# Gate projections of tiles 12 to 23 as 2x2 blocks of seven products, with the pieces of a two-layer hybrid decoder step placed anew

## What is computed

```
h = rmsnorm(x, norm_g)
proj = h @ w_in                     # columns are split into
qkv_a, z_a, beta, alpha, f_b, z_b, qkv_c, z_c, gate_raw = split(proj)
o_a = gated_delta(qkv_a, ...) * silu(z_a)     # branch A
o_b = rwkv7(f_b, ...) * silu(z_b)             # branch B
o_c = block_attention(qkv_c, cache) * silu(z_c)   # branch C
up = einsum(stack(o_a, o_b, o_c), w_branch)
gates = sigmoid(gate_raw + b_gate)            # 3 x 1024 columns
x = x + sum_over_branches(gates * up) @ w_out
x = x + sigmoid(x @ w_pg + b_pg) * (ple @ w_ple)
```

## Time and profile before

| | |
|---|---|
| Median of three runs | 1141.0 us (1139.41 to 1143.78) |
| The profiled execution | 1139.07 us, its span 1137.2 us |
| TensorE busy | 1111.2 us, 98% of the span |
| VectorE busy | 647.6 us, 57% |
| ScalarE busy | 343.8 us, 30% |
| Chain that ended last, by engine | TensorE 86%, VectorE 8% |
| Granted TensorE clock, mean | 0.999 |

### The profile page before, as it was taken

One profiled execution on the slowest core, in us unless ns is written; L12 is line 12 of the kernel. 1 busy time (PEld: TensorE's weight loads), 2 busy tenths in 40 slices (PEclk: granted clock), 3 DMA queues, 4 the chain that ended last, 5 costly groups with the idle time before them and its releaser, 6 DMA issues.

```text
span 1137.2 us, 22007 instructions
## 1 busy us (share of the span) xinstructions
PE 1111.2 (98%) x8504; PEld 867.1 (76%) x8504; DVE 647.6 (57%) x1478; ACT 343.8 (30%) x773; POOL 129.4 (11%) x215
## 2 busy tenths in 40 slices
PE   7999999999999999999999999999999999999998
PEld 6778777768777777779977777777777777777897
DVE  4566546766666505257556673766667643251856
ACT  1243223321334154210323332233224332433013
POOL 0211402020211000000011123201102011000000
PEclk9999999999999999999999999999999999999999
DMA  8733236422513674444346331654134157634431
GB/s 262 222 112 117 56 99 209 104 76 62 121 46 93 205 258 149 152 155 129 106 149 191 105 99 43 191 160 93 39 90 136 39 138 248 198 121 153 145 111 43
DMA packets 162323, 148.51 MB, mean 131 GB/s; under 512 B 41513, under 2 KB 144527, under 8 KB 162029
## 3 DMA queue, kind: packets, MB, share of 16 engines
q1 hardware_dynamic: 156820, 135.99, 40.1%
q0 software_dynamic: 2848, 7.79, 2.1%
q10 hardware_dynamic: 2552, 3.32, 0.9%
HBM read 135.42 MB, written 11.07 MB: 129 GB/s over the span
## 4 chain that ended last, share of the span: by engine, by line
PE 86%; DVE 8%; issue 2%; DMA 2%; ACT 1%; SPq 1%; DVEq 0%; ACTq 0%
PE psum L1250 51%; PE psum L1291 10%; PE psum L1178 5%; PE psum L1480 1%; PE psum L1463 1%; PE psum L1338 1%; PE psum L1599 1%; DMA arena<-conv_in 1%; PE psum L1865 1%; PE psum L1814 1%; PE psum L1683 1%; DVE arena L2641 1%; DVE arena L2796 1%; PE psum L1844 1%; PE psum L1699 1%
## 5 line engine op out<-in xcount | busy, mean ns | idle before, releaser
L1250 PE MATMUL psum<-x_a,ring 128*128 128x288 f32 x1120 | 293.7, 411 | 0.0
L1250 PE MATMUL psum<-x_b,ring 128*128 128x288 f32 x1120 | 293.7, 411 | 0.0
L1250 PEld LDWEIGHTS psum<-x_b,ring 128*128 128x128 f32 x1120 | 205.0, 190 | 59.1 <-issue 8.4
L1250 PEld LDWEIGHTS psum<-x_a,ring 128*128 128x128 f32 x1120 | 205.0, 190 | 59.1 <-issue 8.4
L1950 ACT ACTIVATE arena<-psum 128x512 f32<-128x512 f32 (+7 forms) x181 | 78.1, 451 | 171.0 <-PE psum L1178 61.7
L1250 PE MATMUL psum<-z,ring 128*128 128x288 f32 x384 | 97.6, 407 | 0.0
L1250 PEld LDWEIGHTS psum<-z,ring 128*128 128x128 f32 x384 | 71.4, 190 | 20.3 <-issue 2.3
L1950 ACT ACTIVATE arena<-arena 128x256 f32<-128x256 f32 (+9 forms) x102 | 44.6, 465 | 52.8 <-DVE arena L2689 17.4
L1178 PE MATMUL psum<-consts,arena 128*128 128x128 f32 (+2 forms) x362 | 53.7, 281 | 6.8 <-DMA arena<-in_x_prompt 4.7
L1178 PEld LDWEIGHTS psum<-consts,arena 128*128 128x128 f32 (+2 forms) x362 | 42.8, 146 | 21.6 <-issue 7.4
L1950 ACT ACTIVATE triangles<-psum 128x512 f32<-128x512 f32 (+2 forms) x48 | 24.7, 515 | 78.4 <-PE psum L1463 56.9
(11 more groups left out here) (440 smaller groups left out, 1740.4 us busy)
## 6 DMA issues: line engine op xcount, KB each, us to landing
ring<-in_w_in SPq DMA_DIRECT2D x72, 1024.0 KB, 5.3
ring<-in_w_branch SPq DMA_DIRECT2D x12, 1024.0 KB, 6.1
arena<-in_cache_k SPq DMA_DIRECT2D x32, 256.0 KB, 3.1
arena<-in_cache_v SPq DMA_DIRECT2D x32, 256.0 KB, 3.2
ring<-in_w_out SPq DMA_DIRECT2D x8, 1024.0 KB, 5.2
ring<-in_w_pg SPq DMA_DIRECT2D x8, 1024.0 KB, 5.1
arena<-in_state_dn SPq DMA_DIRECT2D x8, 512.0 KB, 8.3
out_dn_sample<-arena POOLq DMA_DIRECT2D x8, 512.0 KB, 5.0
```

What stands on the lines that cost most here:

```text
L1250: ins = mm(out[:, 0:NTOK], lhs, rhs(k), start=k == 0, stop=k == k_tiles - 1)
```

## The change

Gate tiles 12 to 23 (pairs 6 to 11) leave `project` and are formed as the output projections are: seven products a pair (`gate_product`), each of four 128x144 matmuls, in the order 1, 5, 6, 2, 7, 3, 4. Each product is cut into two pieces of two matmuls. Per layer:

- on TensorE 12 tiles of eight 128x288 matmuls go, 6 x 7 products of four 128x144 matmuls come;
- on VectorE come four token differences of 128x576 (`g_diff`), four weight sums of 128x512 a pair (`g_sum`, the third and fourth written into the ring's slot itself) and two additions of 128x144 a pair (`w_g`, for products 7 and 3);
- on ScalarE two evictions of 128x288 a pair go, and four of 128x144 (products 5, 6, 2 and 4) and one `seed` of 128x144 come;
- the three banks have fixed parts: 1 and 2 in bank 0, 5 and 3 in bank 2, 6, 7 and 4 in bank 1.

The sums of pair q+1 stand among the products of pair q. The token differences lie in the buffer of the triangles, the first two sums in `tmp` and `tanh_z`. So `params_load` of layer 1 now also waits for the last product before it loads into the triangles, and `norm` clears one corner of them in both layers. The filler list changes its order (pairs 6 to 9, then `p_up` of branch B, then pairs 10 and 11), and all of `FILL` is new; it holds 680 entries for 684 filler steps, before 658 for 662.

```diff
+GATE_PAIRS = range(6, 12)
+GATE_BANK = {1: 0, 2: 0, 5: 2, 3: 2, 6: 1, 7: 1, 4: 1}
...
-    for m in range(8):
-        whole("p_g", 8 + m)
-    out.append(("g_tanh", 1, 0))
-    for m in range(4):
-        whole("p_g", 16 + m)
+    def product(q, i):
+        out.append(("half", "w_g", q, i))
+        out.append(("w_g", q, i))
+
+    def gate_pair(q, ahead):
+        product(q, 1)
+        out.append(("seed", "w_g", q))
+        out.append(("g_sum", q, 4))
+        product(q, 5)
+        product(q, 6)
+        if ahead:
+            out.append(("g_sum", q + 1, 1))
+        product(q, 2)
+        if ahead:
+            out.append(("g_sum", q + 1, 2))
+        product(q, 7)
+        product(q, 3)
+        if ahead:
+            out.append(("g_sum", q + 1, 3))
+        product(q, 4)
...
-FILL = [17, 0, 19, 0, 2, 0, 1, 36, 0, 6, 6, 0, 0, 10, 5, 5, 5, 14, 0, 4, 2, 0, 18, 6, 1, 0, 0, 4, 3, 0, 1, 3, 0, 3, 0,
+FILL = [15, 0, 21, 1, 0, 0, 2, 26, 19, 8, 0, 0, 0, 8, 4, 0, 6, 14, 1, 8, 2, 1, 16, 4, 0, 1, 4, 3, 6, 0, 0, 2, 0, 2, 0,
...
+            def gate_product(l, q, i, js):
+
+                c, w = weights(("w_g", l, q))
+                b = GATE_BANK[i]
+                if js[0] == 0:
+                    if i == 1:
+                        pe.wait_ge(S.sem(f"ring{c % RING}_loaded"), 16 * (c // RING + 1))
+                    pe.wait_ge(S.sem(f"bank{b}_read"), S.count(f"bank{b}_read", S.at - 1))
+                    if i == 6:
+                        pe.wait_ge(S.sem("bank0_read"), S.count("bank0_read"))
+                    if i in (5, 6, 7, 3):
+                        pe.wait_ge(S.sem("sums"), S.count("sums", pos[("g_sum", l, q, {5: 1, 6: 2, 7: 3, 3: 4}[i])]))
+                    if i in (5, 6, 7, 4):
+                        pe.wait_ge(S.sem("h_ready"), S.count("h_ready", pos[("g_diff", l, {5: 1, 6: 2, 7: 3, 4: 4}[i])]))
...
+            def w_g(l, q, i):
+                m, part_ = {2: (2 * q, 0), 6: (2 * q, 1), 4: (2 * q + 1, 0), 5: (2 * q + 1, 1)}.get(i, (0, 0))
+                if m == 0:
+                    return
+                gate_free(l, m)
+                b = GATE_BANK[i]
+                fn(gate(m)[:, HALVES[part_]], PS[:, b, 0:HALF], ACT.Identity, scale=0.5, bias=Phalf("b_gate", m)).then_inc(S.sem(f"bank{b}_read"), 1)
...
+                if i == 4:
+                    dve.wait_ge(S.sem("projected"), S.count("projected", pos[("w_g", l, q, 1)]))
+                dst, one, two, op = ((GATE_SUMS[1], w[:, :, 0, 1], w[:, :, 1, 1], ADD), (GATE_SUMS[2], GATE_SUMS[1], w[:, :, 0, 0], SUB),
+                                     (w[:, :, 0, 1], w[:, :, 0, 0], w[:, :, 0, 1], SUB), (w[:, :, 0, 0], w[:, :, 1, 0], GATE_SUMS[2], SUB))[i - 1]
+                tt(dst, one, two, op).then_inc(S.sem("sums"), 1)
```

More of the change, by code:

```diff
@@ L123 @@
     "ple_read": {"p_ple": (1, None)},
-    "sums": {"p_up": (1, lambda st: st[2] == 2 and st[3] in (2, 4, 6)), "w_y": (1, lambda st: st[-1] in (1, 6, 7, 5)),
+    "sums": {"g_sum": (1, None), "p_up": (1, lambda st: st[2] == 2 and st[3] in (2, 4, 6)), "w_y": (1, lambda st: st[-1] in (1, 6, 7, 5)),
              "w_pg": (1, lambda st: st[-1] == 1 or st[-1] in (6, 7, 5) and st[2] < 3)},
@@ L228 @@
     "decay_rate": {"params": (1, None)},
[L229 removed]
+    "h_ready": {"g_diff": (1, None), "norm": (8, None), "params_t": (8, lambda st: st[1] == 0), "x_out": (1, lambda st: st[1] + 1 < DEPTH), "p_up": (4, lambda st: st[2] == 2 and st[3] % 2 == 1), "w_y": (lambda st: (4 if st[2] == 3 else 2) if st[-1] == 3 else 1, lambda st: st[-1] == 3 or st[-1] in (6, 2) and st[2] > 0)},
     "hist_in": {"a_hist": (1, None)},
@@ L291, in banks @@
             where[i] = bank_of(*st[-2:])
+            read = () if st[-1] == 1 else (where[i],)
+        elif st[0] == "w_g":
+            where[i] = GATE_BANK[st[-1]]
             read = () if st[-1] == 1 else (where[i],)
@@ L654, in weight_chunks @@
             continue
-        if kind in PAIRS:
+        if kind == "w_g":
+            a = OFF_G + 256 * st[-2]
+            tile(i, st[:-1], w_in[l, :, :, a:a + 256], KT_, 0, 256)
+        elif kind in PAIRS:
             a = 256 * st[-2]
@@ L2506, in p_up, with g_diff, g_sum, w_g @@
                             dve.wait_ge(S.sem("h_ready"), S.count("h_ready") - 3 + i)
+            def g_diff(l, i):
+                if i == 1:
+                    dve.wait_ge(S.sem("corrected"), S.count("corrected", pos[("b_u", l, 1, 1)]))
+                else:
+                    dve.wait_ge(S.sem("h_ready"), S.count("h_ready") - 1)
+                b11, b12, b21, b22 = (half_tokens(H(l), x, h) for x in range(2) for h in range(2))
+                of, less = ((b12, b11), (b22, gate_tokens(1)), (b22, b12), (b21, gate_tokens(2)))[i - 1]
+                tt(gate_tokens(i), of, less, SUB).then_inc(S.sem("h_ready"), 1)
+            def g_sum(l, q, i):
+                c, w = weights(("w_g", l, q))
+                if i == 1:
+                    dve.wait_ge(S.sem(f"ring{c % RING}_loaded"), 16 * (c // RING + 1))
+                else:
+                    dve.wait_ge(S.sem("sums"), S.count("sums") - 1)
+                if i < 3 and q > GATE_PAIRS[0]:
+                    dve.wait_ge(S.sem("projected"), S.count("projected", pos[("w_g", l, q - 1, {1: 5, 2: 6}[i])]))
+                elif i == 1:
+                    dve.wait_ge(S.sem("b_done"), S.count("b_done", pos[("b_norm6", l, 1, 1)]))
+                elif i == 2:
+                    dve.wait_ge(S.sem("z_done"), S.count("z_done"))
+                if i == 4:
[3 more added lines that the diff above has]
+                tt(dst, one, two, op).then_inc(S.sem("sums"), 1)
+            def w_g(l, q, i):
+                if i not in (7, 3):
+                    return
+                b, other = GATE_BANK[i], {7: 5, 3: 6}[i]
+                name = f"bank{GATE_BANK[other]}_read"
+                dve.wait_ge(S.sem("projected"), S.count("projected"))
+                dve.wait_ge(S.sem(name), S.count(name, pos[("w_g", l, q, other)]))
+                part_ = gate(2 * q + (i == 7))[:, HALVES[1]]
+                stt(part_, PS[:, b, 0:HALF], 0.5, part_, MUL, ADD).then_inc(S.sem(f"bank{b}_read"), 1)
             def weight_sums(n, i):
```

64 lines of the change are left out of this document (49 added, 15 removed), and 12 rows, old and new, of the table FILL.

## The result

The changed kernel takes 1158.96 us (median of 4 runs, 1157.23 to 1160.35), the kernel before 1142.35 beside it (4 runs): a ratio of 1.0151, 95% interval 1.0133 to 1.0170. It is slower by some 17 us. The forecast was 1145, its range ended at 1151; the change lies 8 us above it.

A forecast was written before the change was run, and what follows sets the result against it. TensorE, busy 98% of the span, was taken as the bound. 1139.07 us profiled, less 10.8 saved, plus 15.0 of waits made 1143.3; 1.9 to the median gave 1145 us, forecast's own range 1141 to 1149, overall 1131 to 1151.

The forecast's parts named there:

- What bounds the kernel: Whole kernel: TensorE, busy for 98% of the span; only less work for it or fewer waits can help.
- The saving: TensorE, gate pairs 6 to 11: seven products replace 16 full matmuls, 0.90 us less a pair, 10.8 us in two layers.
- Rival 3: Among mixer steps a product costs more than 0.98 us, by 0.1 each: 8.4 us, 1153 us; chance 0.02.
- The step that failed: Branch C: the granted clock stays at 1.00, since no wait is longer than some gaps are now.
- Term 1: Spread of `c_rope(1)`: 30 pieces ahead instead of 33, 1.5 us more wait a layer, 0.8 to 3.0.
- rival 2: SyncE's stores push the row swaps back, up to 1.5 us a layer at `c_rope(1)`: 1148 to 1151 us; chance 0.24.
- Branches A and B: The same pieces dealt anew there: 0 us, with 2 us to either side.
- Term 2: `c_past(0)` to `c_sprob(0)`: product 5's eviction and pair 8's seed in the queue, 2.0 us wait a layer, 1.3 to 2.4.
- Term 3: `c_score(0,0)` to `c_prob(0,0)`: pair 9's seed stands ahead of the exponentials, 1.4 us wait a layer.
- term 4: `c_past(1)` to `c_sprob(1)`: product 2's eviction stands ahead of the exponential, 1.8 us wait a layer, 1.5 to 2.0.
- term 5: `c_spv(1)` and `c_sout(1)`, one piece of cover each: 0.4 us each, together 0.8 us a layer.
- The sums: VectorE's weight sums, issued four or five products ahead of use: nothing; only pair 6 up to 0.4 us a layer.

The follow-up runs named there:

- e4: Kernel before with seven pieces moved from just ahead of `c_rope(1)` to just behind it; 1151.51 us, ratio 1.0061 to 1.0131 to before.
- e7: Changed kernel with `c_sq` moved ahead of `p_up 0 0`, so SyncE issues the row swaps ahead of the third ring load and the sixteen stores; 1145.45 us.
- v6: e1 with the row swaps issued earlier, and product 2's eviction on ScalarE done at product 3; 1139.28 us, ratio 0.9967 to 0.9999 to before.
- e5: e1 with the additions of `g_sum` 1, 2 and 4 done a second time into unused columns; 1148.95 us, ratio 1.0050 to 1.0089 to before.
- e1: Changed kernel with the places (`FILL`) of before up to `c_rope(1)`, so only branch C's products are new; 1142.59 us, ratio 0.9998 to 1.0047 to before.
- e2: Changed kernel with the places of before from `b_fin(1)` to `c_rope(1)` alone; 1155.43 us, ratio 1.0076 to 1.0147 to before.
- e3: Kernel before with the change's places (`FILL`) up to `c_rope(1)` and no gate product; 1154.51 us, ratio 1.0087 to 1.0143 to before.
- v7: Another execution of v6's own kernel, nothing changed, taken for its profile alone; no median given, 3.4 us lost to the clock.

## Why the prediction was wrong

**What bounds the kernel** held: TensorE's work and waits, with all of the loss in them.

**The saving** held in the main. 10.8 us were forecast, busy time fell by 10.2 once the clock is taken out, and products stand 0.98 us apart (409.59, 410.57 in the changed kernel). Not all of the 10.2 is theirs. In the stretches that hold products, from the spread to the end of the layer, busy time without the clock's share fell by 3.1 us in layer 0 and 3.2 in layer 1. Beside the products the changed kernel has two full pieces there in each layer, and the kernel before had 95 of the 96 that they replace; three pieces at 0.485 us make up 1.5 us a layer. So the products saved some 9 us, an estimate from these figures, and the rest fell where nothing but the places had changed. Rival 3 falls with it. So does, for float32 at 144 columns, the rule of the Trainium skill that was weighed there (TensorE: Matmul & The Clock Gate, "Back-to-back issue gap"): by it a product would have taken up to 1.4 us, an estimate.

**The step that failed** is the sentence that the granted clock stays at 1.00, "since no wait is longer than some gaps are now". I had priced each wait at its own length. Behind the waits of 4.17 and 3.96 us TensorE ran at its 1.2 GHz level, which cost 7.1 us, and 3.2 more behind waits of 2.54 and 2.93 us in branch B: 10.3 of the 21.4. e4 shows it with nothing but a wait, e7 takes wait and clock away together at the spread. The longest gap that I could have pointed to in mid-kernel was 1.62 us. From the 1143.3 us forecast for the profiled execution to its 1160.35 it is 17 us: 10.3 of clock, 6.3 of waits in branches A and B, 0.6 less saved and 0.6 of short idle times, less 0.6, since the waits of branch C and those at start and end came out that much lower.

**Term 1** took three pieces off the cover, 1.5 us, and left the swaps' issue to rival 2. Both happened: from issue to spread it was 2.8 us less in layer 0 and 3.0 in layer 1. 1.5 of each are the pieces; the other 1.3 and 1.5 I put down to the stores, by the unbroken queue ahead of the swaps, and no run shows them apart. In layer 0 VectorE also started 0.75 us later after the issue. The wait grew by 3.5 and 3.0 us where 1.5 was forecast and 3.0 the upper end. Rival 2 had the mechanism, at 1148 to 1151, and even it lacked what follows such a wait.

**Branches A and B** were taken at 0 with 2 us to either side, since before they show few waits. They cost 6.3 us of waits: VectorE's triangles are waited for 1.00 and 0.97 us in each layer, where the trace before has no such wait over 0.32. The pieces before were placed so that few waits were left there; dealing them anew had one likely sign, and I gave it none.

**Terms 2 to 5** were too high, 6.0 us a layer for 3.8; with two waits that no term had (0.73 us in layer 0 ahead of pair 6's first product, 0.23 in layer 1) it is 4.5 and 4.1. Term 2 is 1.10 at `c_sprob(0)` (0.40 and 0.70) and 0.19 ahead of `c_past(0)`, its lower end and not 2.0: three chains in one queue overlapped rather than added. Term 3 is 0.98 for 1.4, term 4 is 1.35 for 1.8, with the cause named rightly (v6), term 5 is 0.19 for 0.8. With the spread the waits of branch C grew by 14.7 us against 15.0 forecast; that match is luck, since term 1 was half its size and the others too large.

**The sums** cost nothing in the change, as forecast: no product waits for one. In e5 even the doubled ones hold up the first pair alone.

What stays open: no run separates branch B's own waits from the lower clock near 328 and 898 us in the changed kernel. None tells why the clock falls at `bs_s0` in one execution and not in the next.

## What to carry to other kernels

A wait on TensorE isn't priced at its length: look how long the longest wait in mid-kernel is, and where a change makes one of several microseconds, count the lower clock behind it too. When work is dealt anew between the steps of a chain, ask of each cover how long it is after the issue of the transfer that starts the chain, and what stands ahead of that issue in its queue; here one item moved ahead of sixteen stores was worth 13.5 us. And a saving of 10 us on the bounding engine is only worth what the waits leave of it: before it is built in, compare it with the old placement kept as it is (e1).

## What the hardware showed

- Behind waits at the spread of 3.4 to 4.5 us the granted clock fell in all seven cases profiled (1.7 to 4.3 us lost each). Behind shorter ones it fell in some: 1.6 us were lost behind 2.12 in e1 and behind 2.55 in e5, none behind 2.02 in e2 nor behind 2.87 in e3. So the length of a wait alone doesn't tell the loss. The Trainium skill (TensorE: Matmul & The Clock Gate, "Part 1: The HAM clock gate") says that the lower level is the default state, released by activity; the traces agree as far as the fall behind idle time goes.
- The clock also fell at `bs_s0`, with TensorE busy for 8.06 of 10 us, mostly in small matmuls of 64x64, behind a wait of 1.62 us (v7's window 320 to 330), and in another execution of the same kernel (v6) it didn't.
- The scatter of one kernel's times goes with the clock. Of 35 executions of the kernel before, 14 had a mean granted clock of 0.999 or 1.000 and took 1136.64 to 1139.66 us; the other 21, at 0.994 to 0.998, took 1138.90 to 1146.46. Where in the execution they lost it is known for the profiled ones alone.
